# Neighbouring pairs of heads together in three mixers, and the first conv chunk stacked through memory

## The reference

```
# band: 12 heads of 64, chunked attention        (memory attention: 4 heads of 64)
s = q·k * scale + bias;  p = softmax(s);  o = p·v;  x = x + concat(o, mem_out) @ w_out

# swa: z = h @ w_in;  u, gate (512 channels each), q (8 heads), k, v (2 heads)
a = u * sigmoid(gate);  y[t, ch] = sum_{j<31} a[t-30+j, ch] * w[j, ch] + b   # depthwise
a_out = silu(layernorm(y));  b_out = sliding-window attention with a sink logit per head
out = concat(a_out, b_out) @ w_out

# fox: 16 heads;  s = q·k/8 + c_t - c_s  (c = cumsum of log sigmoid gates), causal softmax
out = o @ w_out

# behind a mixer of block two:  x = x + rmsnorm(out, g3);  next stage works on rmsnorm(x, g4)
```

## Time and profile before

| what | value |
|---|---|
| runs of the kernel before | 1599.63, 1599.32, 1598.85 us (median 1599.32) |
| profiled execution: its time, its span | 1599.74 us, 1598.0 us |
| busy: PE, DVE, ACT, POOL | 99%, 68%, 58%, 4% of the span |
| chain that ended last | PE 97%, DMA 1%, ACT 1% |
| PE clock granted | full in all of the 40 slices |

### The profile page before, as it was taken

How to read it: one execution, slowest core, us unless ns; L and a number is a source line. 1 busy time by engine, 2 the same in 40 slices (tenths; PEclk the granted TensorE clock), 3 DMA queues, 4 the chain that set the end, 5 groups by cost and what they waited for, 6 DMA issues and landing times.

```text
span 1598.0 us, 23594 instructions
## 1 busy us (share of the span) xinstructions
PE 1587.4 (99%) x9256; PEld 1354.9 (85%) x9256; DVE 1092.2 (68%) x1759; ACT 919.5 (58%) x1555; POOL 56.2 (4%) x96
## 2 busy tenths in 40 slices
PE   9999999999999999999999999999999999999998
PEld 7898888889788888888887788888888889888887
DVE  5986867778677768656677466567565667775665
ACT  6766645567655546545476664447444484664544
POOL 4000000000030000000002100000000000000000
PEclk9999999999999999999999999999999999999999
DMA  8545675554355565566655555655666564356662
GB/s 299 146 146 189 217 238 192 186 174 144 118 193 190 175 199 179 188 197 189 191 159 161 143 191 186 196 185 171 210 185 188 181 200 146 119 184 199 184 189 75
DMA packets 212401, 287.67 MB, mean 180 GB/s; under 512 B 11100, under 2 KB 180382, under 8 KB 212292
## 3 DMA queue, kind: packets, MB, share of 16 engines
q1 hardware_dynamic: 208676, 280.00, 55.3%
q0 software_dynamic: 3616, 6.17, 1.4%
HBM read 284.47 MB, written 3.87 MB: 180 GB/s over the span
## 4 chain that ended last, share of the span: by engine, by line
PE 97%; DMA 1%; ACT 1%; issue 0%; SPq 0%; DVE 0%; POOL 0%; DVEq 0%; ACTq 0%
PE two L2216 91%; PE two L2293 1%; PE two L2462 1%; PE two L2475 1%; PE two L2485 1%; PE two L2870 0%; DMA vals<-u_dram 0%; PE two L2279 0%; PE two L2488 0%; DMA raw<-in_mem_w_kv 0%; PE two L2626 0%; DMA raw<-in_ffn_w_up 0%; DMA u_dram<-aux 0%; PE two L2456 0%; PE two L2844 0%
## 5 line engine op out<-in xcount | busy, mean ns | idle before, releaser
L2216 PE MATMUL two<-act_parts,w_hi 128*128 128x512 f32 (+1 forms) x2784 | 801.7, 353 | 0.0
L1488 DVE TENSOR_TENSOR w_lo<-raw,w_hi 128x1024 fp32r<-128x1024 f32 (+1 forms) x520 | 613.1, 1221 | 105.8 <-ACT w_hi L870 105.6
L2216 PE MATMUL two<-act_parts,w_lo 128*128 128x256 f32 x2256 | 635.0, 281 | 0.0
L2216 PEld LDWEIGHTS two<-act_parts,w_hi 128*128 128x128 f32 x2784 | 487.0, 188 | 81.1 <-issue 5.3
L870 ACT CAST w_hi<-raw 128x1024 fp32r<-128x1024 f32 (+1 forms) x522 | 516.6, 1046 | 5.5 <-DMA raw<-in_ffn_w_up 5.0
L2216 PEld LDWEIGHTS two<-act_parts,w_lo 128*128 128x128 f32 x2256 | 425.5, 189 | 2.1
L2216 PE MATMUL two<-w_hi,act_parts 128*128 128x512 f32 (+2 forms) x832 | 248.6, 378 | 1.5 <-ACT w_hi L870 1.2
L999 ACT COPY p_sb<-two 128x512 f32<-128x512 f32 x108 | 62.4, 578 | 247.1 <-PE two L2216 247.1
L2216 PE MATMUL two<-w_hi,hid_even 128*128 128x512 f32 x576 | 187.8, 393 | 0.0
L2216 PEld LDWEIGHTS two<-w_hi,act_parts 128*128 128x128 f32 x832 | 150.2, 188 | 33.4 <-issue 3.6
L1616 DVE TENSOR_TENSOR pt_sb<-two,p_sb 128x512 f32<-128x512 f32 x54 | 37.3, 691 | 198.4 <-ACT p_sb L999 198.4
(11 more groups left out here) (318 smaller groups left out, 1198.8 us busy)
## 6 DMA issues: line engine op xcount, KB each, us to landing
raw<-in_ffn_w_up SPq DMA_DIRECT2D x160, 512.0 KB, 3.9
raw<-in_ffn_w_down SPq DMA_DIRECT2D x132, 512.0 KB, 3.5
raw<-in_ffn_w_gate SPq DMA_DIRECT2D x80, 512.0 KB, 3.7
raw<-in_a_w_in SPq DMA_DIRECT2D x24, 512.0 KB, 4.3
raw<-in_fox_w_in SPq DMA_DIRECT2D x20, 512.0 KB, 3.8
raw<-in_ffn_w_up SPq DMA_DIRECT2D x32, 256.0 KB, 3.5
raw<-in_w_kv SPq DMA_DIRECT2D x12, 512.0 KB, 3.8
raw<-in_a_w_out SPq DMA_DIRECT2D x8, 512.0 KB, 3.8
```

The source lines that it names most:

```text
L1488: nc.vector.tensor_tensor(w_lo[:, r, 0:n], raw[:, r, 0:n], w_hi[:, r, 0:n], ALU.subtract).then_inc(lo_done, 1)
L2216: return nc.tensor.matmul(dst, a, w, start=start, stop=stop, skip_group_check=True)
```

## The change

1. *swa.* Chunk 0 is turned, written and read back like the other three; the matmuls against the shifted identity, their copies and the tile `shift` go. `turn_u(0)` and `turn_u(1)` stand together; even chunks are copied by DVE, odd ones by ACT. In PE's list scores, turns and values of neighbouring pairs move next to each other, and `swa_out(1, 0)` ahead of `conv(2)`.
2. *band and fox.* In PE's list the same grouping; the lists of ACT and DVE are reordered to suit.
3. *fox to FFN 5.* `arrive` gets an argument `late`. DVE's low parts of slots 456 and 457, which stood ahead of `arrive`, move into it: 456 behind the first residual, 457 to where `arrive` calls `splits(first + 3)`, behind the second half of `normed_lo`. ACT's rounding of both moves behind the first moments.

The core of the diff follows; like moves in fox's loop over m, in ACT's lists and in swa's out projection are left out. POOL's list, and DVE's copy of a turned chunk (it did odd chunks, it does even ones now; ACT's is alike, the other way round) with DVE's list in swa:

```diff
-            pool.wait_ge(pad_out, 16 * (CCH - 1))
+            pool.wait_ge(pad_out, 16 * CCH)
+            write_u(0)
             write_u(1)
+            read_stacked(0)
             read_stacked(1)
...
             def take_turned_u(c):
-                dve.wait_ge(u_full, c)
+                dve.wait_ge(u_full, c + 1)
                 nc.vector.tensor_copy(cv[:, c, :], bank[3][:, 0:SEQ]).then_inc(u_taken[c], 1)
...
             take_u(0, 1)
+            take_turned_u(0)
             splits(282)
-            take_turned_u(1)
             o_lo("swa", 0)
-            copy_stacked(0, 0)
             scores("swa", 2)
             o_lo("swa", 1)
             take_u(1, 0)
-            copy_stacked(0, 1)
             splits(284)
-            scores("swa", 3)
             probs("swa", 2)
             splits(285)
             take_u(1, 1)
-            take_turned_u(3)
+            scores("swa", 3)
+            take_turned_u(2)
             probs("swa", 3)
```

PE's list in swa:

```diff
-            project("GU1", 0, {3: [lambda: turns("swa", 0)], 6: [lambda: turns("swa", 1), lambda: turn_u(1), lambda: values("swa", 0)]})
-            stack(0)
+            project("GU1", 0, {3: [lambda: turns("swa", 0)], 6: [lambda: turn_u(0), lambda: turn_u(1), lambda: turns("swa", 1), lambda: values("swa", 0)]})
             scores("swa", 2)
             values("swa", 1)
-            stack(1)
-            project("GU1", 1, {3: [lambda: scores("swa", 3)]})
+            project("GU1", 1)
+            scores("swa", 3)
             conv(0, 0, QUADS // 2)
             turns("swa", 2)
             turn_u(2)
             turn_u(3)
             conv(0, QUADS // 2)
             conv(1)
-            values("swa", 2)
             turns("swa", 3)
             mean(0)
             mean(1)
+            values("swa", 2)
             values("swa", 3)
...
             swa_out(0, 0, 0)
+            swa_out(1, 0)
             conv(2)
```

PE's list at the end of band, then ACT's there:

```diff
-            values("band", 6)
             turns("band", 7)
             band_out(3, 1)
             band_out(5, 0)
+            values("band", 6)
+            values("band", 7)
             band_out(4, 1)
-            values("band", 7)
+            band_out(5, 1)
             band_out(6, 0)
             band_out(7, 0)
-            band_out(5, 1)
             out_end("band", band_ready, 1)
...
             exps("band", 7)
-            splits(139)
-            o_hi("band", 6)
             pt_copy("band", 7)
             splits(140)
+            o_hi("band", 6)
             o_hi("band", 7)
```

PE's list at the end of fox, DVE's there, and `arrive` of DVE:

```diff
             turns("fox", 7)
+            fox_out(4, 1)
             values("fox", 6)
-            fox_out(4, 0)
             values("fox", 7)
             fox_out(5, 0)
             out_end("fox", pair_ready("fox", 0), 0)
-            for i in range(4, NCH - 2):
-                fox_out(i, 1)
+            fox_out(5, 1)
             out_end("fox", pair_ready("fox", 0), 1)
...
             o_lo("fox", 6)
-            splits(454)
             o_lo("fox", 7)
-            splits(457)
-            arrive(EV["fox"], 5)
+            splits(455)
+            arrive(EV["fox"], 5, late=456)
...
-            def arrive(e, key, tail=True):
+            def arrive(e, key, tail=True, late=None):
...
                 residual(e, 0)
+                if late:
+                    splits(late)
```

More of the change, by code:

```diff
@@ L543, in build @@
         u_full = sem("u_full")
[L544 to L549, removed]
+        u_taken = [sem(f"u_taken{c}") for c in range(CCH)]
+        u_out = [sem(f"u_out{c}") for c in range(CCH)]
+        stacked_in = [sem(f"stacked_in{c}") for c in range(CCH)]
         cv_mu = sem("cv_mu")
@@ L759, in _ @@
             pool.wait_ge(pool_clear, 2)
-            for c in range(1, CCH):
+            for c in range(CCH):
                 pool.dma_start(u_dram[c * P:(c + 1) * P, 0:UPAD], c_wide[:, 0, 0:UPAD]).then_inc(pad_out, 16)
@@ L1446, in _ @@
             splits(435)
-            for m in range(4):
+            for m in range(3):
                 t = fox_slots(m, 0)
                 splits(t + 8)
-                if m == 3:
-                    o_hi("fox", 5)
+                if m:
+                    o_hi("fox", 2 * m - 2)
                 exps("fox", 2 * m)
-                if m in (1, 2):
+                if m:
+                    pt_copy("fox", 2 * m - 1)
+                splits(t + 9)
+                if m:
                     o_hi("fox", 2 * m - 1)
-                splits(t + 9)
                 exps("fox", 2 * m + 1)
                 pt_copy("fox", 2 * m)
-                splits(t + (11 if m == 3 else 10))
-                pt_copy("fox", 2 * m + 1)
-                o_hi("fox", 2 * m)
+                splits(t + 10)
+            t = fox_slots(3, 0)
+            splits(t + 7)
+            o_hi("fox", 4)
+            pt_copy("fox", 5)
+            exps("fox", 6)
+            o_hi("fox", 5)
+            splits(t + 8)
+            exps("fox", 7)
+            pt_copy("fox", 6)
+            splits(t + 9)
+            splits(t + 10)
+            pt_copy("fox", 7)
+            splits(t + 11)
+            o_hi("fox", 6)
+            o_hi("fox", 7)
             splits(455)
-            o_hi("fox", 7)
-            splits(457)
-            arrive(EV["fox"], 5, ACT.Silu)
+            arrive(EV["fox"], 5, ACT.Silu, late=457)
             ffn(5, False)
@@ L2186, in _ @@
             take_pair(0, 1)
-            for m in range(4):
+            for m in range(3):
                 t = fox_slots(m, 0)
-                if m:
-                    o_lo("fox", 2 * m - 2)
                 splits(t + 8)
@@ L2780, in _ @@
             scores("band", 2)
+            scores("band", 3)
             values("band", 1)
             band_part("K1", bank[4], 1)
-            scores("band", 3)
             band_part("K2", bank[5], 0)
@@ L2789, in _ @@
             turns("band", 3)
-            values("band", 2)
             project("VB", 0)
             turns("band", 4)
+            values("band", 2)
             values("band", 3)
@@ L2938, in _ @@
             mean(3)
-            for b in range(NTB):
-                swa_out(1, b)
-            variance()
-            for i in range(2, 4):
-                for b in range(NTB):
-                    swa_out(i, b)
+            swa_out(1, 1)
+            out_chunk("swa", swa_ready, 2, 0, (0,))
+            variance()
+            out_chunk("swa", swa_ready, 2, 0, (1,))
+            swa_out(2, 1)
+            for b in range(NTB):
+                swa_out(3, b)
             for b in range(NTB):
```

124 lines of the change are left out of this document (54 added, 70 removed).

## The result

The changed kernel took 1603.36 us (median of 8 runs, 1600.24 to 1606.32), the kernel before 1599.26 in the same series: a ratio of 1.0025, interval 1.0016 to 1.0034. A second series gave 1602.91 against 1598.90, 1.0029 (1.0018 to 1.0041). So it is 4 us slower; I had forecast 1597.3, and the range ended at 1600.0.

What follows compares the result with a forecast made beforehand. PE, busy 99% of the span, was taken as the bound. Terms swa -3.2, band -1.5, fox -0.7 and behind fox +3.4 sum to -2.0 us: 1597.3 us on the median, range 1595.0 to 1600.0.

Steps and rivals of the forecast that it cites:

- What bounds the kernel: Whole kernel: PE is busy 99% of the span, so each mixer's gain or loss passes whole to the end.
- Prices and band: Each change of tile shape costs 0.18 us; band saves six, and a 0.2 wait by slot 139's rounding goes: -1.5 us.
- rival 4: Small new waits of pairs now standing together, copies having half a us of cover: 0.5 to 2 us, chance 0.07.
- Fox: In fox, 29 changes of tile shape become 25, at 0.18 us each: -0.7 us, no new waits.
- steps 1 and 2: In swa, PE's stacks go for one more turned chunk, net -2.00 us; fewer shape changes give about -0.35.
- Step 3: In swa, conv(2)'s 1.4 us wait for chunk 2 falls to about 0.5, its write 1.8 us earlier: -0.9 us.
- step 4: In swa, chunk 0's new path through memory lands about 866.0, conv(0) due at 867.5: slack some 1.5 us, no term.
- Rival 2: In swa, memory is late and conv(0) waits 2 us for chunk 0; time 1599.3 us, chance 0.15.
- Behind fox: At the arrival behind fox, PE waits for slot 457's low part, made behind normed_lo's second half: +3.4 us.
- Rival 3: The clock falls to half in the stall behind fox: 2.1 to 5.4 us lost, middle 1601.0 us, chance 0.08.

Runs made afterwards that it cites:

- e3: The kernel before with the band and fox changes alone, slot 457's low part right behind that of 456, swa as before: 1597.21 us, ratio 0.9986.
- e6: The kernel of e1 with SP holding its load of slot 288 and all behind it until chunk 1's reads have landed: 1597.32 us, ratio 0.9992.
- e10: e6 with SP also holding FFN 3's first loads (slot 290 and behind) until chunk 2's reads have landed: 1597.06 us, ratio 0.9991.
- e9: The kernel of e1 without chunk 0's four reads, its convolution working on chunk 1's data: 1598.32 us, ratio 1.0000.
- e1: The changed kernel with slot 457's low part made right behind that of 456, not behind both halves of normed_lo: 1599.32 us, ratio 1.0000.
- e12: The changed kernel run again, unaltered, for a second profile: the profiled execution took 1602.30 us.
- e7: e5 and e6 together, on the kernel of e1: 1600.71 us, ratio 1.0011.
- e8: The kernel of e4 with six small DVE copies ahead of slot 457's low part, for a longer stall: 1606.72 us, ratio 1.0047.
- e5: The kernel of e1 with chunk 0's four reads issued from SP's queue instead of POOL's: 1603.55 us, ratio 1.0027.
- e4: The kernel before with only the low parts of slots 456 and 457 made late, as in the changed kernel: 1604.22 us, ratio 1.0031.
- e2: The kernel before with the change in swa alone; band, fox and the arrival behind fox as before: 1601.86 us, ratio 1.0014.

## Why the prediction was wrong, point by point

1. *What bounds the kernel* was right: the last FFN's piece is 167.82 us again, and each stage's gain or loss passes to the end.
2. *Prices and band.* Forecast -1.5, measured -1.5 in the trace, though with a new wait of 0.4 us for probabilities inside (rival 4's kind); with fox, e3 gives -2.0 of the -2.2 forecast for both. Right. That an ACT copy ahead of slot 139's rounding ends a wait there was not tested apart.
3. *Fox.* Forecast -0.7, the trace shows -0.6.
4. *swa, the list of PE and the wait for chunk 2.* PE's list was right: without the waits of the convolution, swa between its landmarks went from 470.5 to 468.3 us, -2.2 where steps 1 and 2 have -2.35. Step 3 was not. Chunk 2's write did come earlier, by 2.0 us beyond what PE had gained ahead of swa (I took 1.8), but it took 5.9 instead of 3.88, so that the reads were no earlier by that count. That no wait for chunk 2 is seen is no gain: chunk 1's hides it. With chunk 1 in time it is 1.5 us (e6) or 0.6 (e10, the weights held longer), and swa gains 1.8 or 2.0, not 3.2.
5. *swa, step 4, the new path of chunk 0: this step failed.* I followed chunk 0's reads to conv(0), gave them 1.5 us of slack and called it no term; conv(0) indeed didn't wait in the changed kernel's profile, but by luck: the last of the four, issued at 859.2, took 5.9 us and landed some 0.1 ahead of it, and in e6 and e10 conv(0) waits 0.4 and 0.8. I did not follow *chunk 1's* reads, which stand behind them in POOL's list, though they now start at 859.9 as before, with four transfers ahead still landing and PE some 4 us further on; and I left out SP's queue, which moves with PE: the slots that GU1 frees come 3 to 4 us earlier, so 512 KB loads run beside the reads. e9 and e6 show the two causes apart: four reads with the early weights land 3 us later than before, which would still be in time for conv(1), eight without the weights cause no wait in conv(1), eight with them are 3.3 to 4.1 us late for it. So swa gave 0.1 us where I had 3.2: this step is half of the 6 us between forecast and median. Rival 2 named late memory, with its place wrong, at 2 us and 0.15.
6. *Behind fox.* Forecast 3.4; the wait measured 3.2 and the stage lost 3.5. Right in mechanism and size: e1, which makes that low part in time, is 4.0 us faster than the changed kernel, the wait and, by the runs' mean clocks, the clock that falls behind it in some of them.
7. *Rival 3, the clock, was under-rated at 0.08: the other step that failed.* The forecast has the clock as no term, and it costs about 2.5 us of the median. I leaned on the kernel's end, where the clock held for 3.9 us into the idle time, and on a stall that was shorter. The runs have two stalls of over 3 us, and behind either the clock falls in some executions and not in others. In the profiles it fell behind 3.1 us (e9), 3.3 (e12), 3.7 (e7), 4.1 (e1), 5.2 (e8) and in 7.1 (e5), and did not fall behind 3.2 (slot 457 in the changed kernel, e12 and e4), 3.3 (e2) and 3.5 (the changed kernel). What decides it between near-equal stalls is open. The price per fall, 1.4 (e12), 1.7 (e1) and 2.8 us (e8), lies below or at the low end of the 2.1 to 5.4 that I took from the start. My reading of the start itself was weak: the window there shows a granted clock of 1.00 in the kernel before, so the slow transposes of the earlier trace rows are no evidence of a lower grant.

```profile
0.00:4.00 4.00, 2.36 (x11) 2.34 (x12) 0.00 (x0) 1.49 (x2) 2.85 (x12) 1.00 0.47 152
```

The sum of what the trace shows, -0.5 - 1.5 - 0.1 - 0.6 + 3.5 = +0.7 with rounding, is the profiled execution; its first term is not the change. With the clock as high as there in all runs the changed kernel would stand near 1600.4 (spans of 1598.5 to 1599.5 and the 1.7 us outside them). Of the further 2.5 to 3 us of the median about 2.5 are clock, as the spans by mean clock show, the rest is time outside the span, whose cause is open. Profiles show the fall itself only behind a wait of the convolution and behind the longer stall of e8.

The Trainium skill ("TensorE: Matmul & The Clock Gate", section "HAM oscillation — how this bites in real kernels") states that waits between bursts of matmuls send the array back to half rate. The falls in e12, e1, e9, e7 and e8 agree; the stalls of 3.2 to 3.5 us without a fall do not, and there the measurement decides. I should have given the rule a chance nearer to a half.

From what the Trainium skill states of a GpSimd transfer ("DMA: Bandwidth & Descriptors", section "Anatomy of one DMA — SWDGE (gpsimd) path") the estimate for 142 KB is 2.3 us. The traces don't agree: chunk 1's reads took 2.8 to 4.9 us before the change and up to 11.8 beside the weights.

## What to carry to other kernels

Work that PE gives up frees slots earlier, and the loads behind them start earlier too: ask which small transfers they will now meet. When a transfer is added to a queue, follow the ones behind it to their own deadlines, not the new one alone. A wait that disappears behind a new one is not a gain: it comes back when the new one is removed. A stall of PE of some 3 us can cost half as much again through the clock in some executions, so a short one that gains were meant to pay for is worth removing first.

## What the runs showed of the hardware

- Four shifted reads of 142 KB (rows of 1136 bytes, each 4 bytes on from the last copy) took 4.7 us at the median from POOL's queue with no weights beside them (e6); the same four from SP's queue, beside four of POOL's, began at 857.3 and let conv(0) start only at 869.5, also without weights (e7).
- Writes of 128 KB to memory took 2.0 us alone and 5.4 beside weight loads (chain of e6).
- Behind near-equal stalls of PE (3.1 to 3.5 us) the granted clock fell in some executions and not in others, and the changed kernel has a spread of 6 us in eight runs where the kernel before has 1.5.
